# Moving the first prompt tile's load, norm and transposes one stage earlier in a streaming-encoder step

## The chip, the cores and the metric

The kernel is one launch on one core of a Trainium2 chip. The metric is device time in microseconds (us). Five engines run side by side, each with its own queue of instructions in program order: TensorE (PE in the profile; PEld is its weight load), VectorE (DVE), ScalarE (ACT), GpSimd (POOL) and SyncE (SP), which here only issues transfers. An engine waits on semaphores that other engines and transfers raise.

## The reference, cut to what matters

One layer runs on a prompt of 2048 tokens and on a sample of 8 sequences of 16 tokens. Width is 1024, all in float32. The change lies in the second of the three steps of the layer, the attention into 256 memory tokens:

```
def memory_attend(h, mem_k, mem_v, w_xq, w_xo):
    q = (h @ w_xq).reshape(B, T, X_HEADS, X_HEAD_DIM)
    s = jnp.einsum('bqhd,bkhd->bhqk', q, mem_k.astype(q.dtype)).astype(jnp.float32) * (X_HEAD_DIM ** -0.5)
    p = jax.nn.softmax(s, axis=-1).astype(q.dtype)
    o = jnp.einsum('bhqk,bkhd->bqhd', p, mem_v.astype(q.dtype)).reshape(B, T, D_MODEL)
    return o @ w_xo

    x = x + memory_attend(rms_norm(x, g_xattn), mem_k, mem_v, w_xq, w_xo)
    x = x + hier_moe(rms_norm(x, g_ffn), w_rg, b_rg, w_re, b_re, w_eg, w_eu, w_ed)
```

The prompt has one pair of key and value arrays (computed in this launch); the sample has a cached pair for each of its 8 sequences. After the attention each token goes to 2 of 32 experts.

## The kernel before, in words

Tokens are cut into 17 tiles of 128 (NT = 17): tile 16 (PT) is the sample, tiles 0 to 15 are the prompt. The program is a row of stages, each a block in which all five engines run their own code; between stages stands a barrier (L113 to L116), which no engine passes before all have arrived. In order:

- stage **a** (L204): token mixing of all tiles; its result x1 is written to DRAM (`x1_d`, x_scratch in the profile);
- stage **q** (L921): folds the prompt's keys and values into two matrices A and B, and makes the sample's queries;
- stage **s** (L1049): the sample's attention. The cached keys of 8 sequences are loaded, transposed on PE (`turn_keys`, into `psa` and `psb`), copied out by ACT (L1106) and DVE (L1127) and used in `scores(0)` after four sequences and `scores(1)` after eight. The softmax follows on DVE and ACT, then transposes of the probabilities (L1186), `values(0)`, `values(1)` (L1172), and transposes of the result (L1193), which ACT copies to `qT` (L1117). SP issues eight 1 MB key loads (two in stage q), then four value loads, each of which waits for `kb_psum` since it reuses a key buffer, and after `scores(1)` the last four, which land in the buffers of the transposed keys;
- stage **r** (L1220): attention of the prompt, residual, norm, and routing of all 17 tiles in the order `ORDER` (the sample is index 0, prompt tile 0 is index 1). It is a software pipeline over steps s. For index i: SP loads x1 (`load_n`, L1292), ACT squares and sums it (L1395), POOL makes 1/sqrt (`rms1`, L1357 and L1359), ACT scales (L1398, `norm`), PE transposes (`turn_h2`, L1596), DVE applies the gain (`h2T_out`, L1459), and PE multiplies with A (`scores`, L1587, two halves), softmax on DVE and ACT (`exps`, L1414), `turn_p` (L1579) and `residual` (L1613);
- the experts, and the last norm.

Before step s = 0 of stage r the pipeline is filled with the front part of index 1:

```
                    pe.wait_ge(S["iotas"], 3)
                    turn_h2(1)
                    for s in range(NT + 3):
```

and in the same way `norm(1)` on ACT, `rms1(1)` on POOL, `h2T_out(1)` on DVE. At step 0 PE has nothing to do; at step 1 it has `scores(1, 0)`, `turn_h2(2)`, `scores(1, 1)` and `residual(0)`. The index 0 tile needs no norm here, since stages q and s have done its attention.

Of the kernel before, what the change touches and what calls it, by code (L numbers as in the profile page):

```python
# [20 lines left out]
I32 = mybir.dt.int32  # L21
# [5 lines left out]
P = 128  # L27
# [69 lines left out]
def build(nc, I, O):  # L97
# [20 lines left out]
    with top:  # L118
# [929 lines left out]

        with one_stage() as st:  # L1049
# [12 lines left out]
            rc = sb("s_rc", [P, HEADS])  # L1062
            psa = pb("s_psa", [P, 8, P])
# [5 lines left out]
                                            "exp_done rc_done prob_done pT_psum pT_done oT_done").split()}  # L1069
            with nc.Block() as block:  # L1070
                @block.sync
                def _(sp):
                    for i in range(2, SEQS):
                        need(sp, S["kb_psum"], i - 3)
                        load_cache(sp, "cache_mem_k", i, raw[i % 4], key_here[i])
                    for i in range(4):
# [3 lines left out]
                    for i in range(4, SEQS):  # L1080
                        load_cache(sp, "cache_mem_v", i, late[i % 4], value_here[i])

                @block.gpsimd
                def _(pool):
                    pool.memset(only[:], 0.0).then_inc(S["zeroed"], 1)

# [9 lines left out]
                def _(act):  # L1096
# [5 lines left out]
                    for i in range(SEQS):  # L1102
# [3 lines left out]
                        act.activation(KTs[i % 4][:, :, 0:P], psa[:], ACT.Copy).then_inc(S["ka_done"], 1)  # L1106
                    act.wait_ge(S["nb_done"], 1)
# [12 lines left out]
                def _(dve):  # L1120
# [10 lines left out]
                    dve.tensor_scalar(nb[:], mx[:], -SCALE, None, ALU.mult).then_inc(S["nb_done"], 1)  # L1131
                    dve.wait_ge(S["exp_done"], 1)
# [9 lines left out]
                def _(pe):  # L1142
# [39 lines left out]
                    scores(1)  # L1182
                    pe.wait_ge(S["prob_done"], 1)
# [4 lines left out]
                    pe.wait_ge(S["pT_done"], 4)  # L1188
                    values(0)
# [5 lines left out]

        e_stack = ExitStack()
        sbe, _, seme = alloc(e_stack)
        gate_here = seme("gate_here")
        up_here = seme("up_here")
        down_here = seme("down_here")  # L1200
        bidx = sbe("p_bidx", [P, 1])
        first_row = sbe("p_first_row", [P, LANES])
        last_row = sbe("p_last_row", [P, LANES])
        zero = sbe("p_zero", [P, EPL])
        prio = sbe("p_prio", [P, NE])
        load = sbe("p_load", [P, 4, NE])
        slot_base = sbe("p_slot_base", [1, EPL], I32)
# [11 lines left out]
        ORDER = [PT] + list(range(PT))  # L1219
        with one_stage() as st:  # L1220
            sb, pb, sem = alloc(st)
            x1n = [sb(f"r_x1n{i}", [P, D]) for i in range(2)]
# [3 lines left out]
            h2T = [sb(f"r_h2T{i}", [P, KD, P]) for i in range(2)]  # L1226
# [846 lines left out]
```

## Time and profile before

| | us |
|---|---|
| median of 3 runs | 2686.27 (2686.26 to 2688.2) |
| the profiled execution, its own time | 2679.83 |
| its span, first to last instruction | 2678.2 |
| PE busy in it | 2451.4 (92%) |
| stages q (end) and s, 1004 to 1060 | PE busy 39.83 of 56.00 |
| stage r and the planning of the experts, 1060 to 1645 | PE busy 544.83 of 585.00 |
| experts, 1645 to 2590 | PE busy 930.33 of 945.00 |

All times of the trace are counted from the start of the span. A row of a timeline merges neighbouring instructions of one line: its start, the time from the first start to the last end, and in brackets the idle time before it with what ended it. The clock of PE is given as a share of 2.4 GHz: 1.00 is 2.4 and 0.50 is 1.2 GHz.

### The profile page before, as it was taken

The page shows a single profiled execution, that of the slowest core. Times are in us where ns is not written, and L with a number is a line of the kernel's source. Part 1 is how long each engine was busy: PE and PEld are TensorE (multiplying, and loading weights), DVE is VectorE, ACT ScalarE, POOL GpSimd, SP SyncE. Part 2 cuts the span into 40 slices and gives each one's busy share as a digit, 9 for nine tenths or more (in the row PEclk, how much of TensorE's full clock was granted, in tenths as well). Part 3 has the DMA queues.
Part 4 walks back from the last instruction along what each step waited for, and adds up shares of the span by engine and source line. Part 5 has one row for each costly group of instructions (what it writes and reads, how often), then busy time and mean ns, then how long its engine had stood idle before and what let it go on. Part 6 is the DMA issues. An engine that isn't in the chain of part 4 may idle for free. (4 is left out here: it accounts for less than half of the span.)

```text
span 2678.2 us, 31438 instructions
## 1 busy us (share of the span) xinstructions
PE 2451.4 (92%) x9509; PEld 1128.8 (42%) x9510; DVE 843.9 (32%) x2292; ACT 466.7 (17%) x945; POOL 718.5 (27%) x657
## 2 busy tenths in 40 slices
PE   8889999999969695999999995999999999999990
PEld 4444444444434374455555542333333333333330
DVE  1484757566556102233333322011111111111113
ACT  2122222122111022222222211000000000000002
POOL 2354554546434000011111011222222222222224
PEclk9999999999989898999999996999999999999995
DMA  6201110110132407322211134947776479979927
GB/s 217 95 28 59 36 59 35 56 38 36 56 153 102 151 1 275 134 71 69 74 63 63 48 104 164 330 142 235 224 243 220 151 232 324 311 242 312 327 78 282
DMA packets 154265, 390.94 MB, mean 146 GB/s; under 512 B 20738, under 2 KB 21274, under 8 KB 154186
## 3 DMA queue, kind: packets, MB, share of 16 engines
q1 hardware_dynamic: 128178, 339.39, 35.4%
q0 software_dynamic: 19040, 45.23, 7.0%
q10 hardware_dynamic: 6976, 5.42, 0.6%
q8 instruction: 39, 0.64, 0.1%
q14 instruction: 32, 0.26, 0.0%
HBM read 323.53 MB, written 66.70 MB: 146 GB/s over the span
## 5 line engine op out<-in xcount | busy, mean ns | idle before, releaser
L738 PE MATMUL a_psz<-W 128*128 128x512 f32 x1088 | 484.4, 599 | 1.3 <-ACT W L497 1.3
L594 DVE SCALAR_TENSOR_TENSOR yacc<-aext,pcol,yacc 128x256 f32<-128x256 f32 x928 | 369.9, 476 | 0.0
L738 PEld LDWEIGHTS a_psz<-W 128*128 128x128 f32 x1088 | 205.3, 193 | 239.5 <-issue 239.5
L1936 PE MATMUL e_psg<-W,e_xT 128*64 x672 | 298.4, 597 | 3.2 <-DMA W<-in_w_expert_gate 2.2
L1936 PE MATMUL e_psy<-W,e_hT 128*64 x672 | 297.2, 595 | 3.6
L1937 PE MATMUL e_psg<-W,e_xT 128*64 128x512 f32 x672 | 298.4, 597 | 0.0
L1937 PE MATMUL e_psy<-W,e_hT 128*64 128x512 f32 x672 | 297.4, 595 | 0.0
L1937 PE MATMUL e_psu<-W,e_xT 128*64 128x512 f32 x672 | 295.2, 592 | 0.0
L1936 PE MATMUL e_psu<-W,e_xT 128*64 x672 | 295.2, 592 | 0.0
L1763 POOL DMA_INDIRECT x_scratch<-e_y,e_stoken x42 | 69.7, 1660 | 672.8 <-DVE e_token L1860 356.0
L453 POOL TENSOR_TENSOR a_vn<-a_vn,gv 128x512 f32<-128x512 f32 x17 | 242.8, 14282 | 15.2 <-ACT a_vn L542 15.2
L1613 PE MATMUL r_psx<-W 128*128 128x512 f32 x544 | 237.7, 595 | 0.0
L1587 PE MATMUL r_pss<-W,r_h2T 128*128 128x512 f32 x512 | 226.8, 596 | 1.4 <-DVE r_h2T L1459 1.4
L1873 DVE TENSOR_TENSOR e_hb<-e_psu,e_sg 128x256 f32<-128x256 f32 x84 | 31.7, 419 | 552.8 <-PE e_psu L1937 509.8
L1936 PEld LDWEIGHTS e_psg<-W,e_xT 128*64 128x64 f32 x672 | 92.6, 138 | 194.0 <-issue 194.0
L1936 PEld LDWEIGHTS e_psu<-W,e_xT 128*64 128x64 f32 x672 | 92.1, 137 | 188.6 <-issue 188.6
L1936 PEld LDWEIGHTS e_psy<-W,e_hT 128*64 128x64 f32 x672 | 88.6, 137 | 178.3 <-issue 178.3
L1613 PEld LDWEIGHTS r_psx<-W 128*128 128x128 f32 x544 | 102.8, 191 | 123.3 <-issue 123.3
L1587 PEld LDWEIGHTS r_pss<-W,r_h2T 128*128 128x128 f32 x512 | 95.6, 192 | 110.6 <-issue 108.7
L906 PE MATMUL a_psz<-W,a_maT 128*128 128x512 f32 x272 | 122.7, 594 | 5.1 <-ACT a_maT L550 5.1
L906 PE MATMUL a_psz<-W 128*128 128x512 f32 x272 | 122.3, 592 | 0.0
L1885 DVE TENSOR_SCALAR e_y<-e_psy,e_spair 128x512 f32<-128x512 f32 x42 | 31.5, 751 | 265.3 <-PE e_psy L1937 265.3
(316 smaller groups left out, 2560.7 us busy)
## 6 DMA issues: line engine op xcount, KB each, us to landing
W<-in_w_expert_gate SPq DMA_DIRECT2D x32, 2048.0 KB, 10.9
W<-in_w_expert_up SPq DMA_DIRECT2D x32, 2048.0 KB, 10.5
W<-in_w_expert_down SPq DMA_DIRECT2D x32, 2048.0 KB, 10.6
W<-in_x_prompt SPq DMA_DIRECT2D x32, 512.0 KB, 3.9
x_scratch<-W SPq DMA_DIRECT2D x18, 512.0 KB, 3.0
r_x1r<-x_scratch SPq DMA_DIRECT2D x17, 512.0 KB, 4.3
x_scratch<-r_x SPq DMA_DIRECT2D x17, 512.0 KB, 2.9
h_scratch<-r_h SPq DMA_DIRECT2D x17, 512.0 KB, 2.9
```

Source lines behind the costliest of these rows:

```text
L453: pool.tensor_tensor(vn[:], vn[:], gv[:], ALU.mult).then_inc(S["vgain"], 1)
L594: ins = dve.scalar_tensor_tensor(out=out, in0=src, scalar=w, in1=yacc[:, i, :], op0=ALU.mult, op1=ALU.add)
L738: last = pe.matmul(psz[bank][:], hT[t.par][:, k, :], w_in[:, k, COL[bank]:COL[bank] + 512], start=(k == 0), stop=(k == KD - 1))
L906: last = pe.matmul(psz[n][:], (maT[:, k, :] if k < CG else mbl[t.par][:, k - CG, :]), w_out[:, k, 512 * n:512 * n + 512], start=(k == 0), ...
L1587: last = pe.matmul(pss[:, 2 * n:2 * n + 2, :].rearrange("p h n -> p (h n)"), h2T[i % 2][:, k, :], A[:, k, 512 * n:512 * n + 512], start=(k ...
L1613: last = pe.matmul(psx[:, 512 * n:512 * n + 512], (pT if i else qT)[:, c, :], (B if i else w_xo)[:, c, 512 * n:512 * n + 512], start=(c == ...
L1763: pool.indirect_dma_start(out=x2_d.rearrange("t p d -> (t p) d"), out_offset=bass.IndirectOffsetOnAxis(ap=stoken[t.par][:], axis=0), in_=y ...
L1873: dve.tensor_tensor(hb[:, c], psu[:, c], sg[:, c], ALU.mult).then_inc(S["h_done"], 1)
L1885: dve.tensor_scalar(yb[t.par][:, 512:1024], psy[:, 512:1024], spair[t.par][:, 1:2], None, ALU.mult).then_inc(S["y_done"], 1)
L1936: pe.matmul(out[0:HALF, :], xt[:, 0:HALF], W[:, bass.ds(base + at, 512)], start=start, stop=stop)
L1937: return pe.matmul(out[HALF:P, :], xt[:, HALF:P], W[:, at:at + 512], start=start, stop=stop)
```

## The change

The front part of index 1 leaves the head of stage r and stands in stage s. `x1n` and `h2T` are allocated ahead of stage s, in a stack of their own (`r_stack`), and live until the end of stage r. SP issues the loads of `x1n` for index 1 and for index 2 in stage s, between the fourth and the fifth key sequence. ACT squares index 1 after its copy for sequence 3 and scales it in place after its copy for sequence 5; POOL makes the 1/sqrt. PE transposes it after `scores(1)` into `pso`, and DVE applies the gain between the negated maximum and the reciprocal of the sums. `values(0)` waits for that, since it writes `pso`. The norm of index 2 stays in stage r. All counts of semaphores in stage r that spoke of index i are lowered by one; `load_n(3)` no longer waits for a norm. The block of expert arrays (`e_stack`) is moved up unchanged.

```diff
+        r_stack = ExitStack()
+        sbr, _, _ = alloc(r_stack)
+        x1n = [sbr(f"r_x1n{i}", [P, D]) for i in range(2)]
+        h2T = [sbr(f"r_h2T{i}", [P, KD, P]) for i in range(2)]
+        ORDER = [PT] + list(range(PT))
...
                     for i in range(2, SEQS):
                         need(sp, S["kb_psum"], i - 3)
                         load_cache(sp, "cache_mem_k", i, raw[i % 4], key_here[i])
+                        if i == 3:
+                            for j in (1, 2):
+                                sp.dma_start(x1n[j % 2][:], x1_d[ORDER[j], :, :]).then_inc(x1n_here[j % 2], 16)
...
                         load_cache(sp, "cache_mem_v", i, late[i % 4], value_here[i])
+                    sp.wait_ge(x1n_here[0], 16)
...
                     pool.memset(only[:], 0.0).then_inc(S["zeroed"], 1)
+                    pool.wait_ge(S["squares"], 1)
+                    settle(pool)
+                    pool.tensor_scalar(rs[:, 0:1], ss[:], EPS, None, ALU.add).then_inc(S["eps"], 1)
+                    pool.wait_ge(S["eps"], 1)
+                    pool.tensor_tensor(rs[:, 1:2], rs[:, 0:1], mhalf[:], ALU.pow).then_inc(S["rstd"], 1)
...
                         act.activation(KTs[i % 4][:, :, 0:P], psa[:], ACT.Copy).then_inc(S["ka_done"], 1)
+                        if i == 3:
+                            act.wait_ge(x1n_here[1], 16)
+                            act.activation(o_tok[:], x1n[1][:], ACT.Square, scale=1 / 32, accum_out=ss[:]).then_inc(S["squares"], 1)
+                        if i == 5:
+                            act.wait_ge(S["rstd"], 1)
+                            act.wait_ge(S["squares"], 1)
+                            act.activation(x1n[1][:], x1n[1][:], ACT.Copy, scale=rs[:, 1:2]).then_inc(S["normed"], 1)
...
                     dve.tensor_scalar(nb[:], mx[:], -SCALE, None, ALU.mult).then_inc(S["nb_done"], 1)
+                    dve.wait_ge(S["h2_psum"], 1)
+                    dve.tensor_tensor(h2T[1][:], pso[:].rearrange("p (k n) -> p k n", k=KD),
+                                      gcol[:, 8:16].unsqueeze(2).to_broadcast([P, KD, P]), ALU.mult).then_inc(S["h2T_done"], 1)
                     dve.wait_ge(S["exp_done"], 1)
...
                     for i in range(4, SEQS):
                         turn_keys(i)
                     scores(1)
+                    pe.wait_ge(S["normed"], 1)
+                    for k in range(KD):
+                        last = pe.transpose(pso[:, P * k:P * k + P], x1n[1][:, P * k:P * k + P], ident[:])
+                    last.then_inc(S["h2_psum"], 1)
                     pe.wait_ge(S["prob_done"], 1)
                     for h in range(HEADS):
                         for m in range(2):
                             last = pe.transpose(psa[:, 2 * h + m, :], prob[:, h, P * m:P * m + P], ident[:])
                     last.then_inc(S["pT_psum"], 1)
                     pe.wait_ge(S["pT_done"], 4)
+                    pe.wait_ge(S["h2T_done"], 1)
                     values(0)
                     values(1).then_inc(S["o_psum"], 1)
...
                     def load_n(i):
-                        need(sp, S["normed"], i - 2)
+                        need(sp, S["normed"], i - 3)
                         sp.dma_start(x1n[i % 2][:], x1_d[ORDER[i], :, :]).then_inc(x1n_here[i % 2], 16)
...
                     load_r(0)
-                    load_n(1)
-                    load_n(2)
                     load_r(1)
                     load_part(sp, EPL, 0, 0, 0)
                     for s in range(NT + 1):
...
                     def rms1(i):
-                        pool.wait_ge(S["squares1"], i)
-                        need(pool, S["normed"], i - 1)
+                        pool.wait_ge(S["squares1"], i - 1)
+                        need(pool, S["normed"], i - 2)
                         settle(pool)
                         pool.tensor_scalar(rs1[:, 0:1], ss1[:], EPS, None, ALU.add).then_inc(S["eps1"], 1)
-                        pool.wait_ge(S["eps1"], i)
+                        pool.wait_ge(S["eps1"], i - 1)
                         pool.tensor_tensor(rs1[:, 1:2], rs1[:, 0:1], mhalf[:], ALU.pow).then_inc(S["rstd1"], 1)
...
-                    rms1(1)
                     for s in range(NT + 3):
                         if s + 2 < NT:
                             rms1(s + 2)
...
                     def norm(i):
-                        act.wait_ge(x1n_here[i % 2], 16 * ((i + 1) // 2 if i % 2 else i // 2))
-                        need(act, S["h2_turned"], i - 1)
-                        need(act, S["rstd1"], i - 1)
+                        need(act, x1n_here[i % 2], 16 * ((i - 1) // 2))
+                        need(act, S["h2_turned"], i - 2)
+                        need(act, S["rstd1"], i - 2)
                         act.activation(xn, x1n[i % 2][:], ACT.Square, scale=1 / 32, accum_out=ss1[:]).then_inc(S["squares1"], 1)
-                        act.wait_ge(S["rstd1"], i)
-                        act.wait_ge(S["squares1"], i)
+                        act.wait_ge(S["rstd1"], i - 1)
+                        act.wait_ge(S["squares1"], i - 1)
                         act.activation(xn, x1n[i % 2][:], ACT.Copy, scale=rs1[:, 1:2]).then_inc(S["normed"], 1)
...
-                    norm(1)
                     for s in range(NT + 2):
...
                     def h2T_out(i):
-                        dve.wait_ge(S["h2_turned"], i)
+                        dve.wait_ge(S["h2_turned"], i - 1)
                         need(dve, S["s_psum"], i - 2)
                         dve.tensor_tensor(h2T[i % 2][:], pst[:], gcol[:, 8:16].unsqueeze(2).to_broadcast([P, KD, P]), ALU.mult).then_inc(S["h2T_done"], 1)
...
-                    h2T_out(1)
                     for s in range(NT + 3):
...
                         if i == 1:
-                            pe.wait_ge(S["h2T_done"], 2)
+                            pe.wait_ge(S["h2T_done"], 1)
...
                     def scores(i, n):
                         if n == 0:
-                            pe.wait_ge(S["h2T_done"], i)
+                            need(pe, S["h2T_done"], i - 1)
                             need(pe, S["exp_done"], i - 1)
...
                     def turn_h2(i):
-                        pe.wait_ge(S["normed"], i)
+                        pe.wait_ge(S["normed"], i - 1)
                         need(pe, S["pT_done"], i - 2)
...
                     def turn_h3(i):
                         pe.wait_ge(S["h3_done"], i + 1)
-                        need(pe, S["h2T_done"], min(i + 3, NT - 1))
+                        need(pe, S["h2T_done"], min(i + 3, NT - 1) - 1)
                         need(pe, S["pT_done"], min(i + 1, NT - 1))
...
                     pe.wait_ge(S["iotas"], 3)
-                    turn_h2(1)
                     for s in range(NT + 3):
                         if 1 <= s - 1 < NT:
                             turn_p(s - 1)
...
+        r_stack.close()
```

**PE, the end of stage s and the start of stage r.** L1193 and L1239 are the last transposes of stage s, the two branches the way through the barrier. Before:

```order
L1160 MATMUL s_pss<-s_KT,s_only 32x256 x3
L1186 MATMUL s_psa<-ident,s_prob 128x128 x8
...
L1193 MATMUL s_psb<-ident,s_otok 128x128 x8
L1070 UNCONDITIONAL_BRANCH
L1570 UNCONDITIONAL_BRANCH
L1596 MATMUL r_pst<-ident,W 128x128 x8
L1587 MATMUL r_pss<-W,r_h2T 128x512 x8
L1596 MATMUL r_pst<-ident,W 128x128 x8
L1587 MATMUL r_pss<-W,r_h2T 128x512 x8
L1613 MATMUL r_psx<-W 128x512 x16
```

The same place of the changed kernel:

```order
L1201 MATMUL s_pss<-s_KT,s_only 32x256 x3
L1226 MATMUL s_pso<-ident,r_x1n 128x128 x8
L1231 MATMUL s_psa<-ident,s_prob 128x128 x8
...
L1239 MATMUL s_psb<-ident,s_otok 128x128 x8
L1092 UNCONDITIONAL_BRANCH
L1595 UNCONDITIONAL_BRANCH
L1612 MATMUL r_pss<-W,r_h2T 128x512 x8
L1621 MATMUL r_pst<-ident,W 128x128 x8
L1612 MATMUL r_pss<-W,r_h2T 128x512 x8
L1638 MATMUL r_psx<-W 128x512 x16
```

Eight transposes have moved from the head of stage r to the place between the last scores and the transposes of the probabilities; the first thing of stage r is now a half of the scores.

**ACT, the middle of stage s.** The copies of the transposed keys (s_psa) of sequences 0 to 7. Before:

```order
L1106 ACTIVATE W<-s_psa 128x8x128
L1106 ACTIVATE s_KT<-s_psa 128x8x128 x3
L1106 ACTIVATE W<-s_psa 128x8x128
L1106 ACTIVATE s_KT<-s_psa 128x8x128 x3
L1109 ACT_TABLE_LOAD
```

Of the changed kernel:

```order
L1137 ACTIVATE W<-s_psa 128x8x128
L1137 ACTIVATE s_KT<-s_psa 128x8x128 x3
L1140 ACTIVATE s_otok,s_ss<-r_x1n 128x1024
L1137 ACTIVATE W<-s_psa 128x8x128
L1137 ACTIVATE s_KT<-s_psa 128x8x128
L1144 ACTIVATE r_x1n<-r_x1n,s_rs 128x1024
L1137 ACTIVATE s_KT<-s_psa 128x8x128 x2
L1147 ACT_TABLE_LOAD
```

The square stands in the pause of the first scores, the scaling between two key copies, and no further table load comes in.

**SP, the transfers of stage s and of the head of stage r.** Before:

```order
L918 DMA W<-in_cache_mem_k 128x2x1024 x6
L918 DMA W<-in_cache_mem_v 128x2x1024 x5
L918 DMA s_KT<-in_cache_mem_v 128x2x1024 x3
L1070 UNCONDITIONAL_BRANCH
L1288 UNCONDITIONAL_BRANCH
L1296 DMA r_x1r<-x_scratch 128x1024
L1292 DMA r_x1n<-x_scratch 128x1024 x2
L1296 DMA r_x1r<-x_scratch 128x1024
L1216 DMA W<-in_w_expert_gate 128x8x512
L1292 DMA r_x1n<-x_scratch 128x1024 x2
```

Of the changed kernel:

```order
L918 DMA W<-in_cache_mem_k 128x2x1024 x2
L1100 DMA r_x1n<-x_scratch 128x1024 x2
L918 DMA W<-in_cache_mem_k 128x2x1024 x4
L918 DMA W<-in_cache_mem_v 128x2x1024 x5
L918 DMA s_KT<-in_cache_mem_v 128x2x1024 x3
L1092 UNCONDITIONAL_BRANCH
L1318 UNCONDITIONAL_BRANCH
L1326 DMA r_x1r<-x_scratch 128x1024 x2
L1249 DMA W<-in_w_expert_gate 128x8x512
L1322 DMA r_x1n<-x_scratch 128x1024 x2
```

Two loads of 512 KB have moved ahead of four key loads and all value loads; in stage r the expert's 2 MB now stands third.

## Rows read from the trace of the kernel before

**Rows 1.** The page, busy time of each engine, share of the span, instructions.

```profile
PE 2451.4 (92%) x9509; PEld 1128.8 (42%) x9510; DVE 843.9 (32%) x2292; ACT 466.7 (17%) x945; POOL 718.5 (27%) x657
```

**Rows 2.** Windows of stage r: length, five busy times, PE clock, DMA share, GB/s.

```profile
1074.01:1083.70 9.69, 9.69 (x24) 4.69 (x25) 0.00 (x0) 1.15 (x1) 0.79 (x2) 0.81 0.32 108
1083.70:1585.00 501.30, 501.30 (x1645) 259.45 (x1644) 157.97 (x516) 117.32 (x272) 51.86 (x86) 1.00 0.20 69
```

**Rows 3.** Timeline of PE across the barrier between stages s and r.

```profile
1057.26 1.09 PE L1193 MATMUL s_psb<-ident,s_otok 128*128 128x128 f32 x8 [0.80 <-DVE s_otok L1139]
1070.65 1.94 PE L1596 MATMUL r_pst<-ident,W 128*128 128x128 f32 x8 [12.30 <-ACT W L1398]
1074.01 8.98 PE L1587 MATMUL r_pss<-W,r_h2T 128*128 128x512 f32 x16 [1.42 <-DVE r_h2T L1459]
1082.83 1.04 PE L1596 MATMUL r_pst<-ident,W 128*128 128x128 f32 x8
1083.70 7.03 PE L1587 MATMUL r_pss<-W,r_h2T 128*128 128x512 f32 x16
1090.57 13.90 PE L1613 MATMUL r_psx<-W 128*128 128x512 f32 x32
1104.30 1.04 PE L1579 MATMUL r_pst<-ident,W 128*128 128x128 f32 x8
```

**Rows 4.** Timelines of ACT and POOL at the head of stage r.

```profile
1067.11 1.06 ACT L1395 ACTIVATE W<-r_x1n 128x1024 f32<-128x1024 f32 x1 [7.70 <-DMA r_x1n<-x_scratch]
1069.36 1.15 ACT L1398 ACTIVATE W<-r_x1n,r_rs 128x1024 f32<-128x1024 f32 x1 [1.10 <-POOL r_rs L1359]
1060.37 0.30 POOL L1333 TENSOR_SCALAR_AFFINE_SELECT r_lower<-ones 128x128 f32<-128x128 f32 x1
```

**Rows 5.** Timeline of ACT in stage s, the copies of sequences 4 and 6.

```profile
1026.85 1.03 ACT L1106 ACTIVATE W<-s_psa 128x1024 f32<-128x1024 f32 x1 [6.22 <-PE s_psa L1147]
1031.39 1.02 ACT L1106 ACTIVATE s_KT<-s_psa 128x1024 f32<-128x1024 f32 x1 [1.25 <-PE s_psa L1147]
```

**Rows 6.** Timelines of DVE and PE in stage s after the last scores.

```profile
1043.46 0.18 DVE L1133 RECIPROCAL s_rc<-s_sm 128x4 f32<-128x4 f32 x1 [2.00 <-ACT s_prob L1109]
1044.96 1.97 PE L1186 MATMUL s_psa<-ident,s_prob 128*128 128x128 f32 x8 [4.98 <-DVE s_prob L1135]
```

**Rows 7.** Timeline of PE, transposes of key sequences 3 and 7.

```profile
1018.50 1.06 PE L1147 MATMUL s_psa<-ident,W 128*128 128x128 f32 x8 [0.19 <-ACT s_KT L1106]
1032.55 1.06 PE L1147 MATMUL s_psa<-ident,W 128*128 128x128 f32 x8
```

**Rows 8.** Transfers: when SP issued the last key load, and its time to landing.

```profile
1020.75 0.38 SPq L918 DMA_DIRECT2D W<-in_cache_mem_k  x1
W<-in_cache_mem_k SPq DMA_DIRECT2D x1, 1024.0 KB, 8.6
```

**Rows 9.** Transfers of stage r: the expert weights, time to landing, and their issue.

```profile
W<-in_w_expert_gate SPq DMA_DIRECT2D x1, 2048.0 KB, 12.8
1062.24 0.44 SPq L1216 DMA_DIRECT2D W<-in_w_expert_gate  x1
```

**Rows 10.** Windows of the transfers in stage s: at full rate, and two pauses.

```profile
1022.00:1026.00 4.00, 3.88 (x67) 2.66 (x68) 0.00 (x0) 0.00 (x0) 0.00 (x0) 1.00 1.04 413
...
1027.50:1029.50 2.00, 1.67 (x15) 1.36 (x14) 1.23 (x1) 0.76 (x2) 0.00 (x0) 1.00 0.41 63
1039.75:1041.75 2.00, 0.23 (x7) 0.00 (x0) 1.39 (x2) 0.25 (x1) 0.00 (x0) 1.00 0.46 47
```

**Rows 11.** Weight loads of the last values, and landing times of all cache loads.

```profile
1052.76 0.14 PEld L1172 LDWEIGHTS s_pso<-W,s_only 128*32 128x32 f32 x2 [0.52 <-issue]
DMA to landing us min/median/max: 4.9/7.1/11.0
```

**Rows 12.** Windows in which the clock of PE fell, and in which it rose.

```profile
1060.50:1060.75 0.25, 0.00 (x0) 0.00 (x0) 0.00 (x0) 0.00 (x0) 0.25 (x2) 0.89 0.00 0
...
1077.75:1078.00 0.25, 0.25 (x2) 0.12 (x1) 0.00 (x0) 0.00 (x0) 0.00 (x0) 0.97 0.57 213
```

More of the change, by code:

```diff
@@ L1047, in build @@
         kv_stack.close()
+        e_stack = ExitStack()
+        sbe, _, seme = alloc(e_stack)
+        gate_here = seme("gate_here")
+        up_here = seme("up_here")
+        down_here = seme("down_here")
+        bidx = sbe("p_bidx", [P, 1])
+        first_row = sbe("p_first_row", [P, LANES])
+        last_row = sbe("p_last_row", [P, LANES])
+        zero = sbe("p_zero", [P, EPL])
+        prio = sbe("p_prio", [P, NE])
+        load = sbe("p_load", [P, 4, NE])
+        slot_base = sbe("p_slot_base", [1, EPL], I32)
+        r_stack = ExitStack()
[3 more added lines that the diff above has]
+        ORDER = [PT] + list(range(PT))
         with one_stage() as st:
@@ L1062, in build @@
             rc = sb("s_rc", [P, HEADS])
+            ss = sb("s_ss", [P, 1])
+            rs = sb("s_rs", [P, 2])
             psa = pb("s_psa", [P, 8, P])
@@ L1068, in build @@
             S = {n: sem("s_" + n) for n in ("zeroed q_only ka_psum kb_psum ka_done kb_done s_psum o_psum o_done oT_psum max_done nb_done "
-                                            "exp_done rc_done prob_done pT_psum pT_done oT_done").split()}
+                                            "exp_done rc_done prob_done pT_psum pT_done oT_done squares eps rstd normed h2_psum h2T_done").split()}
+            x1n_here = [sem(f"s_x1n_here{i}") for i in range(2)]
             with nc.Block() as block:
@@ L1194, in _ @@
                     last.then_inc(S["oT_psum"], 1)
[L1196 to L1207, printed above, removed]
         def load_part(eng, e, base, n, r):
@@ L1217, in load_part @@
                           I[name][0][bass.ds(e, 1), :, :].rearrange("a (k p) n -> p (a k) n", p=P)).then_inc(here, 16)
-        ORDER = [PT] + list(range(PT))
         with one_stage() as st:
             sb, pb, sem = alloc(st)
-            x1n = [sb(f"r_x1n{i}", [P, D]) for i in range(2)]
             x1r = [sb(f"r_x1r{i}", [P, D]) for i in range(2)]
@@ L1225, in build @@
             h3 = [sb(f"r_h3{i}", [P, D]) for i in range(2)]
-            h2T = [sb(f"r_h2T{i}", [P, KD, P]) for i in range(2)]
             h3T = sb("r_h3T", [P, KD, P])
```

## Prediction, before the changed kernel ran

> **What bounds the kernel now.** I began with the page: PE is busy for 2451.4 us, 92% of the span [rows 1], so what counts is where PE waits, and whether it waits again afterwards for what a change moves. The windows say how stage r runs: from 1083.70 to 1585 PE is busy in 501.30 of 501.30 us at the full clock [rows 2]. So whatever lets this stretch begin earlier is worth its full length at its end. The timeline of PE shows what stands ahead of it [rows 3]: the last transposes of stage s end at 1058.35, then PE is idle for 12.30 us, until 1070.65; eight transposes of index 1 take 1.94 us, then comes a wait of 1.42 us for DVE, and the scores begin at 1074.01. The wait's chain is on the other engines [rows 4]: ACT waits 7.70 us for the load of x1, squares at 1067.11, waits 1.10 us for POOL, and scales until 1070.51. Nothing else feeds PE in that time: step 0 of the pipeline has no work for it. The semaphore that PE waits for first, `iotas` at 3, comes from POOL's third instruction, which ends at 1060.67.
>
> **What the change removes at the head of stage r.** PE's first instruction is now `scores(1, 0)`, and its inputs (A and `h2T[1]`) exist. It waits for `iotas` alone. With 0.15 us for the signal, my estimate from the 0.14 us between ACT's end at 1070.51 and PE's start at 1070.65 [rows 3, 4], it starts at 60.67 + 0.15: 1060.82. In stage r only the transposes and the DVE multiply are gone from PE's path; the rest keeps its order.
>
> How long until `scores(1, 1)` starts, which now is at 1083.70? From the start of `scores(1, 0)` it takes 9.69 us now, at a mean clock of 0.81 [rows 2]. At full clock the same work takes 6.87 (the second half, 1083.70 to 1090.57) plus 0.87 (transposes, 1082.83 to 1083.70), 7.74 us [rows 3]; 1.95 us are lost to the slow clock. The slow clock has a cause in the idle time: it fell around 1060.70, 2.3 us after PE's last work, and rose only around 1077.76 [rows 12]. In the changed kernel the idle time is 1058.35 to 1060.82, 2.47 us, just past the moment at which the clock fell. I take it as fallen and keep the same 1.95 us of loss. Then `scores(1, 1)` starts at 1060.82 + 7.74 + 1.95 = 1070.51 instead of 1083.70: 13.2 us earlier. Bounds for the loss: nothing, if the clock stays up (15.1 us gained); and 3.55 us, if it stays down as long after PE's first work as it did now, 1070.65 to 1077.76, 7.1 us at half speed (11.6 us gained). I choose 1.95 because it was measured on the same instructions.
>
> The Trainium skill, in "TensorE: Matmul & The Clock Gate" under "Part 1: The HAM clock gate", says that the clock follows how busy the engine has recently been and that the number of slow matmuls at a start differs from run to run of one kernel. By that rule the loss would not be a fixed 1.95 us, and the case of no loss (a gain of 15.1 us) is open in some runs; the trace agrees in so far as the clock fell 2.3 us after the work ended and rose 7.1 us after it began again.
>
> **What it adds in stage s.** Everything there must fit beside what bounds that stage, and each piece has a gap:
> - ACT, square: 1.06 us and the reading of the sum, 0.2, in an idle time of 6.22 us ahead of the copy at 1026.85 [rows 4, 5]. Its load was issued around 1011, far ahead. Cost nothing; if the load landed after 1025.6, each us late would cost one, since the key copies queue behind it.
> - ACT, scaling: 1.15 us [rows 4] between the copies of sequences 5 and 6. ACT is idle there for 1.25 us, until 1031.39 [rows 5]. It fits by 0.1 us, and the 1/sqrt is made on POOL, idle, 8 us earlier. Cost 0 to 0.1 us.
> - PE, eight transposes: 1.06 us at full clock [rows 7] in the idle 4.98 us before the transposes of the probabilities [rows 6]. Cost nothing.
> - DVE, the gain: the same instruction takes at most the 1.42 us that PE waited for it [rows 3]; it stands after the negated maximum, in an idle time of 2.00 us before the reciprocal at 1043.46 [rows 6]. `values(0)` waits for it, but also for the probabilities, which come later. Cost nothing; without the cover 1.4 us.
> - The transfers: two loads of 512 KB, 1.05 MB, at 413 GB/s [rows 10]: 2.54 us, in front of four key loads. The last key load was issued at 1020.75 and landed 8.6 us later, 1029.35 [rows 8]; PE turned it at 1032.55 [rows 7]. Pushed by 2.54 us it lands at 1031.89, with 0.66 us to spare. The value loads: the transfers had two pauses of 2 us, at 63 and 47 GB/s, around 1028.5 and 1040.7 [rows 10]. Each could carry 1.7 us of full traffic, 3.4 us together, more than the 2.54 us added. So the last four values, which start only after `scores(1)`, aren't delayed. That matters, since they are what bounds the stage: 4.19 MB from 1041.75 at 413 GB/s end at 1051.9, and PE begins `values(1)` at 1052.76 after 0.52 us of idle with no other input missing [rows 11]. It also means that a faster clock for the transposes and `values(0)` would bring nothing here. Cost of the transfers: nothing, at most their full 2.54 us.
>
> The Trainium skill says in "DMA: Bandwidth & Descriptors", under "Queues, rings and completion order", that on each transfer engine the descriptors of one issuing engine are consumed in ring order. By that rule the two keys issued ahead of the new loads aren't touched, and the later ones are pushed by the whole length; its warning, that completions need not come in order, is the way in which a key could be late all the same.
>
> **What it shifts in stage r.** `norm(2)` finds its x1 there and runs at once, on ACT from about 1060.5, long before PE turns it at 1069.6. SP now issues expert weights third and x1 of index 3 behind them. The weights landed at 1062.24 + 12.8 = 1075.04 [rows 9]; without two tiles ahead of them that is 1072.5, and index 3 lands one tile (1.27 us) later, 1073.8. `norm(3)` is queued ahead of the exponentials of index 1 on ACT. It ends 3.40 us later (1067.11 to 1070.51 in [rows 4]), 1077.2; PE finishes the scores at 1070.51 + 6.87 = 1077.38, so the exponentials aren't held up. Behind that PE has the 13.73 us of `residual(0)` [rows 3] before it needs the probabilities at 1091.1. From the negated maximum to the first transpose takes 3.5 us (1041.46 to 1044.96 [rows 6]), which leaves 10.4 us of spare time. Cost nothing.
>
> **Sum.** 13.2 us off the profiled execution's 2679.83 (span 2678.2 and 1.6 around it): 2666.6. That execution was 6.4 us below the median of the runs shown; against the median it is 2686.27 - 13.2 = **2673.1 us**.
>
> **The rivals.**
> - The clock stays up. The idle time of 2.47 us is shorter than any that now precedes a slow stretch; against it stands the fall 2.3 us after the last work. Gain 15.1 us, 2671.1.
> - Key or value loads come late and stretch stage s. For it: only 0.66 us of room at the last key. Against it: the two pauses. Worst case all 2.54 us, gain 10.7 us, 2675.6.
> - The moved work isn't hidden in stage s: 1.25 + 1.15 + 1.06 + 1.42 = 4.9 us on the path, gain 8.3 us, 2678.0. For it the gap of 1.25 us that takes 1.15 us; against it the other three gaps, all at least 0.5 us wider than their work.
> - The change moves a wait and doesn't remove it: something after stage r is paced by transfers and takes the 13 us back, 2686. Against it: every stage starts at a barrier, and no transfer of a later stage is issued ahead of it except by stage r's own steps.
> - Slower: x1 of index 3 is stuck behind the expert weights, ACT stands before it with the exponentials in its queue, and PE waits for the probabilities of index 1. Break-even needs the spare 10.4 us and the 13.2 us gained to be used up: landing at 1073.8 + 23.6 = 1097.4. If it took 30 us longer than forecast, PE would lose 19.6 and the time be 2692.7. The longest landing in this stretch was 12.8 us [rows 9], so this is unlikely.
>
> **How the numbers follow.** Forecast as worked out (gain about 13.2, slow clock for a while) 0.50; clock stays up 0.22; loads late 0.12; work not hidden 0.06; given back 0.07; slower 0.03. A measurement of this kernel tells from no change about 0.2%, 5.4 us. Faster holds the first four, 0.90; same 0.07; slower 0.03. The likeliest case alone spans 2671.1 to 2674.6 by the bounds of the clock. The range goes up to the unhidden work, 2678, and down to 2667, because one execution of the same kernel was already 6.4 us under its median. What lies outside is the two last rivals and some noise.
>
> **What the next profile would show.** Right: PE idle about 2.5 us between stages s and r, then `scores` first, and PE busy without a gap from there to the end of stage r; the last transposes of stage s at 1057.26 as now; `values(1)` still at about 1052.8; a slow clock in the first microseconds of stage r. Wrong: PE waiting for a key transfer before 1032.55, `values(1)` later than 1052.8, ACT's copies of the keys shifted, or an idle time of PE at the transposes of the probabilities around 1091. A start of stage r later than 1060.1 would mean that stage s grew.

## The result and the profile after

The changed kernel took 2665.91 us (median of 4 runs, 2665.3 to 2670.32) beside 2686.27 us (4 runs, 2686.02 to 2688.2): a ratio of 0.9926, 95% interval 0.9909 to 0.9943. That is 20.4 us faster, with an interval of about 15.3 to 24.4 us. Forecast were 13.2 us and a range of 2667 to 2678; the direction was right, the time lies 1.1 us below the range. Its profiled execution took 2666.03 us (span 2664.4), 13.8 us less than that of the kernel before. So the first question is already in these numbers: profile against profile gives 13.8 us, median against median 20.4.

The timeline of PE after the change, the counterpart of [rows 3]:

```profile
1041.41 1.09 PE L1226 MATMUL s_pso<-ident,r_x1n 128*128 128x128 f32 x8
1046.45 1.97 PE L1231 MATMUL s_psa<-ident,s_prob 128*128 128x128 f32 x8 [3.95 <-DVE s_prob L1176]
1049.27 6.76 PE L1213 MATMUL s_pso<-W,s_only 128*32 128x256 f32 x65 [0.85 <-DVE s_only L1124]
...
1060.11 1.09 PE L1239 MATMUL s_psb<-ident,s_otok 128*128 128x128 f32 x8 [0.82 <-DVE s_otok L1180]
1063.62 7.13 PE L1612 MATMUL r_pss<-W,r_h2T 128*128 128x512 f32 x16 [2.42 <-POOL r_lower L1361]
1070.59 1.04 PE L1621 MATMUL r_pst<-ident,W 128*128 128x128 f32 x8
1071.46 7.03 PE L1612 MATMUL r_pss<-W,r_h2T 128*128 128x512 f32 x16
1078.33 13.90 PE L1638 MATMUL r_psx<-W 128*128 128x512 f32 x32
1092.06 1.04 PE L1604 MATMUL r_pst<-ident,W 128*128 128x128 f32 x8
```

The idle time of 12.30 us between the stages is 2.42 us, ended by POOL's third list (r_lower), and the first scores take 7.13 us, where they took 8.98: there is no slow clock here. After that PE never stops in stage r, which the windows show; compare [rows 2]:

```profile
1063.62:1071.46 7.84, 7.84 (x24) 3.96 (x25) 0.00 (x0) 2.12 (x3) 2.23 (x18) 1.00 0.93 320
1071.46:1573.00 501.54, 501.54 (x1648) 259.72 (x1646) 158.16 (x516) 117.16 (x272) 51.74 (x86) 1.00 0.21 73
```

In stage s one row differs from what was forecast: `values(0)` and one matmul behind it (x65) took 6.76 us, where they took 5.40. PE came to the transposes of the probabilities 34.58 us after the stage's start, as before the change (1046.45 less 1011.87, 1044.96 less 1010.38), but began `values(1)` at 1055.66, 43.8 us after it instead of 42.4. And stage r began 2.90 us later in time than in the profile before (1063.05 beside 1060.15): 1.49 us of that come from stages ahead of stage s, 1.41 from stage s. On ACT the timeline shows the moved pieces, and the first thing queued behind a late transfer in stage r:

```profile
1022.02 1.04 ACT L1140 ACTIVATE s_otok<-r_x1n 128x1024 f32<-128x1024 f32 x1
...
1031.53 1.14 ACT L1144 ACTIVATE r_x1n<-r_x1n,s_rs 128x1024 f32<-128x1024 f32 x1
1032.88 1.02 ACT L1137 ACTIVATE s_KT<-s_psa 128x1024 f32<-128x1024 f32 x1 [0.21 <-PE s_psa L1188]
...
1078.00 1.06 ACT L1422 ACTIVATE W<-r_x1n 128x1024 f32<-128x1024 f32 x1 [10.80 <-DMA r_x1n<-x_scratch]
...
1081.33 0.46 ACT L1441 ACTIVATE W<-r_pss,r_nb 128x256 f32<-128x256 f32 x1
```

The scaling of index 1 leaves ACT still 0.21 us of waiting before the next key copy: it fits. The square of index 3 at 1078.00 waited for its tile, and the exponentials of index 1 queued behind it began at 1081.33. PE didn't notice, since `residual(0)` lasts until 1092.06.

And on DVE the gain stands where it was to stand, with time to spare before the reciprocal:

```profile
1042.87 1.22 DVE L1171 TENSOR_TENSOR r_h2T<-s_pso,gcol 128x1024 f32<-128x1024 f32 x1
1044.96 0.18 DVE L1174 RECIPROCAL s_rc<-s_sm 128x4 f32<-128x4 f32 x1 [0.87 <-ACT s_prob L1147]
```

The transfers, as times from issue to landing: the last key load (issued at 1022.24), and x1 of index 3 (issued at 1064.36).

```profile
W<-in_cache_mem_k SPq DMA_DIRECT2D x1, 1024.0 KB, 11.3
r_x1n<-x_scratch SPq DMA_DIRECT2D x1, 512.0 KB, 13.6
```

The last key took 11.3 us instead of the 8.6 in [rows 8], 2.7 more (forecast 2.54), and landed at 1033.54; PE used it at 1034.05.

### The profile page after: what moved, and what is told of

It is laid out like the page before. It is cut to its first block and busy times, and to the rows that moved or that the text cites. A ratio compares the mean times of both kernels' runs of the same rounds, so it can differ in the third digit from the quotient of the medians.

```text
span 2664.4 us, 31438 instructions
## 1 busy us (share of the span) xinstructions
PE 2451.7 (92%) x9509; PEld 1128.0 (42%) x9510; DVE 843.8 (32%) x2292; ACT 465.9 (17%) x945; POOL 717.8 (27%) x657
```

## The experiments

Ten runs. The two theories, as they stand in the expectations: **A**, the change is worth 13 to 16 us at the head of stage r, and the rest of the first result is spread between executions; **B**, it does something more elsewhere.

The table has been worked out from the timelines of each profile. "Stage s" goes from PE's first key transposes to POOL's first list; "head" from there to the second half of the scores of index 1, behind which PE is busy without a pause. "Scores, first half" is the time of PE's first 16 matmuls of these scores; 7.03 us is what such a half takes at the full clock.

| profile | stage s | head | both | scores, first half |
|---|---|---|---|---|
| before | 49.77 | 23.55 | 73.32 | 8.98 |
| before, again (e1) | 50.72 | 24.15 | 74.87 | 9.83 |
| arrays moved only (e3) | 51.03 | 24.38 | 75.41 | 9.93 |
| loads moved only (e4) | 51.12 | 17.97 | 69.09 | 9.59 |
| changed | 51.18 | 8.41 | 59.59 | 7.13 |
| changed, again (e2) | 51.20 | 8.41 | 59.61 | 7.13 |
| changed, third (e8) | 51.08 | 8.41 | 59.49 | 7.13 |
| start held (e5) | 51.18 | 13.96 | 65.14 | 10.14 |
| loads doubled (e6) | 52.88 | 11.45 | 64.33 | 10.17 |
| PE filled once (e7) | 53.83 | 7.83 | 61.66 | 7.11 |
| lists later (e9) | 51.23 | 7.83 | 59.06 | 7.11 |
| PE filled thrice (e10) | 51.09 | 7.83 | 58.92 | 7.10 |

**e1, the kernel before again.** No edit.

> The kernel before, once more, to see how its own executions spread and where the 6.4 us lie between its profiled execution (2679.83) and its median (2686.27). Theory A (the change is worth its 13 to 15 us at the head of stage r, and the rest of the measured 20.4 us is spread of the executions or of the chips): ratio 1.000, and executions at both about 2680 and about 2686 turn up, so that a large sample's median may lie below 2686. Theory B (the change does something more, some 6 us, outside the head of stage r): executions of before keep to 2686, and 2679.83 was an exception.

Measured: 2684.11 us (11 runs, 2679.49 to 2687.15), ratio 0.9996 (0.9987 to 1.0005). Executions near 2680 and near 2687 both turn up: one execution says little to 5 us. Its profile shows that the first one was a favourable draw at the very place of the change:

```profile
1074.13 1.94 PE L1596 MATMUL r_pst<-ident,W 128*128 128x128 f32 x8 [12.04 <-ACT W L1398]
1077.49 9.83 PE L1587 MATMUL r_pss<-W,r_h2T 128*128 128x512 f32 x16 [1.42 <-DVE r_h2T L1459]
1087.16 1.04 PE L1596 MATMUL r_pst<-ident,W 128*128 128x128 f32 x8
1088.04 7.03 PE L1587 MATMUL r_pss<-W,r_h2T 128*128 128x512 f32 x16
```

The first half of the scores lasts 9.83 us, 2.8 us over the 7.03 at full clock, against 1.95 in [rows 3]. The clock fell later here. The window in which it fell:

```profile
1065.50:1066.00 0.50, 0.00 (x0) 0.00 (x0) 0.00 (x0) 0.00 (x0) 0.41 (x4) 0.89 0.42 156
```

PE's last work of stage s ended at 1062.09. A clock of 0.89 as the mean of half a microsecond puts the fall at about 1065.9, 3.8 us behind that work, and not 2.3 us as in [rows 12].

**e2, the changed kernel again.** No edit.

> The changed kernel, once more. Theory A: 13 to 15 us faster than the kernel before on the same chip, ratio about 0.9947. Theory B: about 20 us faster again, ratio 0.9925. In its profile both expect the scores of index 1 to begin some 13 us earlier after the start of stage r than before; the first microseconds may be at the slow or at the full clock.

Measured: 2670.69 us (5 runs, 2668.18 to 2673.64), ratio 0.9947 (0.9933 to 0.9961), 14.5 us between the medians. Head 8.41, full clock. This is A's value, and B's 0.9925 lies outside the interval.

**e3, only the arrays moved.** The kernel before with:

```diff
+        e_stack = ExitStack()
...
+        r_stack = ExitStack()
+        sbr, _, _ = alloc(r_stack)
+        x1n = [sbr(f"r_x1n{i}", [P, D]) for i in range(2)]
+        h2T = [sbr(f"r_h2T{i}", [P, KD, P]) for i in range(2)]
+        ORDER = [PT] + list(range(PT))
```

> Only the allocations of the change: the expert arrays, x1n and h2T are allocated ahead of stage s, all work stays where it was. Theory A: no change, ratio 1.000, PE's idle time at the head of stage r 12.3 us as before. Theory B, in the form that the places of the arrays in memory matter: about 6 us faster, ratio 0.9976, with PE's idle time at that place unchanged.

Measured: 2684.98 us (11 runs), ratio 0.9998 (0.9989 to 1.0007). No effect of the places in memory is seen, and the interval leaves room for 3 us at most; B's form of it (6 us) falls.

**e4, only the loads moved.** As e3, and:

```diff
+                        if i == 3:
+                            for j in (1, 2):
+                                sp.dma_start(x1n[j % 2][:], x1_d[ORDER[j], :, :]).then_inc(x1n_here[j % 2], 16)
...
-                    load_n(1)
-                    load_n(2)
...
```

> The loads of both x1 tiles move to stage s, all computing stays at the head of stage r. ACT can square from 60.5 instead of 67.1, but POOL is at its index lists until 62.2, so the scaled tile is ready at about 64.4, PE transposes until 66.5, and the scores begin near 67.9 instead of 74.0: a gain of 6.1 us by theory A, ratio 0.9977, less than half of the whole change, the rest being compute that only its move hides. A rival in which the load is all that matters (the compute chain hides behind something) would give the full 13 us or more. Stage s should keep its length, apart from the clock of PE.

Measured: 2677.41 us (7 runs, 2674.38 to 2679.92), ratio 0.9971 (0.996 to 0.9982), 7.8 us. The head is 17.97, 6.2 to 6.4 us shorter than in e1 and e3 (forecast 6.1), and stage s as long as in e3: no cost of the 1 MB of loads is seen there. The timeline:

```profile
1066.00 1.94 PE L1603 MATMUL r_pst<-ident,W 128*128 128x128 f32 x8 [6.11 <-ACT W L1405]
1069.36 9.59 PE L1594 MATMUL r_pss<-W,r_h2T 128*128 128x512 f32 x16 [1.42 <-DVE r_h2T L1466]
1078.79 1.04 PE L1603 MATMUL r_pst<-ident,W 128*128 128x128 f32 x8
```

PE still idles 6.11 us and loses 2.56 us to the slow clock (9.59 against 7.03). The other 9.6 us of the head (17.97 to 8.41) come only with the norm and the transposes.

**e5, PE's start in stage r held back.** The changed kernel with:

```diff
                     pe.wait_ge(S["iotas"], 3)
+                    pe.wait_ge(S["rstd1"], 1)
```

> The changed kernel, but PE starts the scores of index 1 only when POOL has made the 1/sqrt of index 2: 2.55 us later than in the changed kernel, after about 5.0 us of idle instead of 2.4. Theory A (the forecast put the loss by the slow clock at the head of stage r too high, because after 2.4 us of idle the clock mostly stays up): here the clock falls, and from the start of the stage to the second half of the scores of index 1 it takes 8.4 + 2.55 plus 1.7 to 3 us of loss, 12.7 to 14 us. Rival (the clock at this place has nothing to do with the length of the idle time): 11.0 us, full clock. Median about 2672 to 2675 for a changed kernel of about 2668.

```profile
1067.31 10.14 PE L1612 MATMUL r_pss<-W,r_h2T 128*128 128x512 f32 x16 [4.96 <-POOL r_rs L1387]
1077.28 1.04 PE L1621 MATMUL r_pst<-ident,W 128*128 128x128 f32 x8
```

Measured: one execution, 2673.54 us; head 13.96, of which 2.54 is the later start and 3.0 the slow clock (10.14 against 7.13). After 4.96 us of idle the clock had fallen. The head lies in A's range (12.7 to 14) and not at the rival's 11.0. It is one execution, and e6 shows that the length of the idle time alone doesn't decide.

**e6, the loads doubled.** The changed kernel; the second copies go to memory that nothing reads at that time, SP waits for them at the end of the stage, and nothing else is changed.

```diff
+        twin = [W[:, 7168:8192], h2T[0][:].rearrange("p k n -> p (k n)")]
...
+                                sp.dma_start(twin[j % 2], x1_d[ORDER[j], :, :]).then_inc(twin_here[j % 2], 16)
```

> The changed kernel with each of the two x1 tiles loaded twice in stage s (the second copy goes to unused memory): 2.54 us more of transfers in front of the same four keys. Theory A (one pair of tiles fits with 0.5 us to spare at the last key and costs nothing): the last key is now about 2 us late, its transposes begin at 24.3 us after the stage's start instead of 22.2, and the stage grows by 2 to 2.6 us. Rival (transfers in stage s never bound the keys, there is more room than it looks): stage s keeps its 51.2 us.

```profile
1033.96 1.09 PE L1193 MATMUL s_psa<-ident,W 128*128 128x128 f32 x8 [1.71 <-DMA W<-in_cache_mem_k]
...
1036.52 1.09 PE L1193 MATMUL s_psa<-ident,W 128*128 128x128 f32 x8 [0.59 <-DMA W<-in_cache_mem_k]
...
1039.07 1.10 PE L1193 MATMUL s_psa<-ident,W 128*128 128x128 f32 x8 [0.58 <-DMA W<-in_cache_mem_k]
...
1068.39 10.17 PE L1617 MATMUL r_pss<-W,r_h2T 128*128 128x512 f32 x16 [2.42 <-POOL r_lower L1366]
```

Measured: one execution, 2676.33 us. Now three key sequences are late; the last one's transposes begin 24.13 us after the stage's first (forecast 24.3, changed kernel 22.2), and the stage grows by 1.7 us (forecast 2 to 2.6; `values(0)`, 5.39 us here, had the full clock earlier). So the room for the keys was as small as the sum said. The last row is a finding of its own: after the same 2.42 us of idle as in the changed kernel, this time the clock had fallen, and the head took 11.45. PE's last work had ended at 1065.97, and the clock fell at about 1067.7, 1.7 us behind it:

```profile
1067.50:1067.75 0.25, 0.00 (x0) 0.00 (x0) 0.00 (x0) 0.00 (x0) 0.00 (x0) 0.91 0.00 0
1067.75:1068.00 0.25, 0.00 (x0) 0.00 (x0) 0.07 (x1) 0.00 (x0) 0.18 (x2) 0.50 0.00 0
```

So equal idle times at this place can end with either clock. This kernel's stage s differs, though, and all three profiles of the changed kernel itself show the full clock: that the changed kernel too loses the 3.04 us in some executions is not shown.

**e7, PE filled once, lists later.** The changed kernel with 24 transposes whose result nothing reads, and the wait for POOL's lists moved to their first use:

```diff
                     last.then_inc(S["h2_psum"], 1)
+                    for j in range(24):
+                        pe.transpose(psb[:, j % 8, :], x1n[1][:, P * (j % 8):P * (j % 8) + P], ident[:])
...
-                    pe.wait_ge(S["iotas"], 3)
...
+                        if i == 0:
+                            pe.wait_ge(S["iotas"], 3)
                         pe.wait_ge(S["picked"], i + 1)
```

> The changed kernel with two additions: 24 idle transposes into a free part of PSUM after those of index 1, so that PE works through most of the softmax's 3.95 us of idle, and the wait for POOL's lists taken from the head of stage r to the first use of those lists. Theory A (in stage s the slow clock after the softmax costs 1.4 us, until the last values' landing bounds it; the lists cost 0.5 us): transposes of the probabilities 1.06 us instead of 1.97, values(0) about 3.6 instead of 6.8, values(1) at about 42.6 us after the stage's start instead of 44.0, stage r's scores 0.5 us earlier; 2.0 us faster than the changed kernel, ratio to before about 0.9938. Rival (the clock doesn't answer to such filling, or the transfers are later than they look): 0.5 us.

```profile
1048.62 1.09 PE L1233 MATMUL s_psa<-ident,s_prob 128*128 128x128 f32 x8 [1.33 <-DVE s_prob L1176]
1050.56 3.66 PE L1213 MATMUL s_pso<-W,s_only 128*32 128x256 f32 x64 [0.85 <-DVE s_only L1124]
1057.74 0.61 PE L1213 MATMUL s_pso<-W,s_only 128*32 128x256 f32 x1 [3.52 <-DMA s_KT<-in_cache_mem_v]
```

Measured: 2671.58 us (5 runs), ratio 0.995 (0.9937 to 0.9963). A miss in sum: 2.0 us faster than the changed kernel was expected, and it is 3.2 us slower in the mean than e8, which was timed with it (5.2 between the medians). By the trace stage s became 2.7 us longer, and the two stages together 2.2 us longer than in e8. The parts say why. Transposes and `values(0)` ran at full clock as expected (1.09 and 3.66 us), so PE came sooner to its wait for the last values. These were ready 43.7 us after the stage's start, not at the 42.6 expected; PE idled 3.52 us and went into `values(1)` with the slow clock (0.61 us for a matmul that takes 0.38 at full clock). The slow spell had only been moved behind the wait. The lists did what was expected: head 7.83.

**e8, the changed kernel a third time.** No edit.

> The changed kernel a third time, beside more executions of the kernel before. Theory A (the change is worth about 15.5 us at the head of stage r, what differs from that in the first result is spread between executions): ratio about 0.9942, 15 to 16 us. Theory B (about 20 us, the second result being the exception): 0.9925.

Measured: 2666.35 us (6 runs, 2665.83 to 2675.38), ratio 0.994 (0.9925 to 0.9955), 16.1 us by the ratio, 18.0 us between the medians. A's 0.9942 is met, but B's 0.9925 is the edge of the interval: here the timing alone doesn't decide, the profile does. The table's three profiles of the changed kernel agree to 0.12 us in stage s and head together.

**e9, lists later alone.** The changed kernel with the last two pieces of e7's edit.

> The changed kernel with only the wait for POOL's lists taken from the head of stage r to the first use of those lists. PE then starts the scores 0.57 us earlier, after 1.86 us of idle instead of 2.42. Theory A (PE's start there is set by that wait alone): from the start of the stage to the second half of the scores 7.8 us instead of 8.4, always at full clock; stage s unchanged at 51.1; 0.6 us faster than the changed kernel by the trace, which the timing can't resolve: ratio to before 0.993 to 0.995. Rival (something else, such as the fetch of the stage's code, holds PE): 8.4.

```profile
1064.72 7.11 PE L1612 MATMUL r_pss<-W,r_h2T 128*128 128x512 f32 x16 [1.87 <-PEq L116]
```

Measured: 2668.52 us (5 runs), ratio 0.9941 (0.9927 to 0.9954). Head 7.83, as forecast, at the full clock: 0.58 us that the timing can't resolve.

**e10, PE filled thrice.** As e9, with `idle_turns(n, ps)`, a loop of n such transposes:

```diff
+                    idle_turns(24, psb)
...
                     values(0)
+                    idle_turns(28, psb)
                     values(1).then_inc(S["o_psum"], 1)
...
                     last.then_inc(S["oT_psum"], 1)
+                    idle_turns(10, psa)
```

> As the one before, and PE is kept at work with idle transposes in three places of stage s: 24 after those of index 1 (softmax), 28 between values(0) and values(1), where the kernel with one filling waited 3.5 us for the last values and lost the fast clock, and 10 after the last transposes of the stage. Theory A (that loss of 2.7 us in stage s was the slow clock after the wait, and nothing but the landing of the last values then bounds the stage): values(1) begin at 42.6 to 43.9 us after the stage's start and run at full clock, 3.5 us instead of 6.9; stage s takes 50 to 51 us instead of 53.9, and the clock never falls between stages s and r. Ratio to before 0.993 to 0.9945. Rival (the filling itself costs, for instance by slowing the transfers): stage s stays above 52 us.

```profile
1046.42 1.09 PE L1236 MATMUL s_psa<-ident,s_prob 128*128 128x128 f32 x8 [1.33 <-DVE s_prob L1176]
1048.36 3.66 PE L1217 MATMUL s_pso<-W,s_only 128*32 128x256 f32 x64 [0.85 <-DVE s_only L1124]
1051.95 3.27 PE L1208 MATMUL s_psb<-ident,r_x1n 128*128 128x128 f32 x28
1055.50 0.38 PE L1217 MATMUL s_pso<-W,s_only 128*32 128x256 f32 x1 [0.27 <-DMA s_KT<-in_cache_mem_v]
...
1062.95 7.10 PE L1619 MATMUL r_pss<-W,r_h2T 128*128 128x512 f32 x16 [0.80 <-PEq L116]
```

Measured: 2666.63 us (5 runs, 2666.03 to 2669.48), ratio 0.9935 (0.9921 to 0.9948). With the wait filled too, `values(1)` run at full clock (0.38 us each) and stage s is back at 51.09. `values(1)` began 43.7 us after the stage's start in e7 and here alike, so the 2.7 us of e7 were the slow clock. It gains nothing over the changed kernel's 51.2, though: PE had to wait for the last values until 1055.50, and they landed about 1 us later in the stage than in the changed kernel (11.9 us after their issue, 10.8 there). It is the best version that was run; its lead over the changed kernel is 0.7 us in the two stages by the trace, within the timing's uncertainty.

## Why the prediction was right or wrong

**The mechanism and the place were right.** PE's chain at the head of stage r was replaced by scores that begin when POOL's third list is there; the 2.42 us of idle stand against 2.47 forecast. From POOL's first list to the first scores it took 13.86, 13.60 and 13.74 us in the profiles of kernels in which no work was moved (before, e1, e3) and 0.57 us in the three of the changed kernel: 13.0 to 13.3 us less, against 13.19 in the forecast. Stages s and head together take 59.6 us in three profiles of the changed kernel, and 73.3, 74.9 and 75.4 in the three of kernels in which no work was moved: a mean of 14.97 us less.

**The term that was mis-sized is the slow clock at the head of stage r.** The prediction kept "the same 1.95 us of loss" on both sides. On the new side the loss is nought in all three profiles of the changed kernel (7.13 us for the first half); that was the rival "the clock stays up", with 0.22. On the old side 1.95 was low: e1, e3 and e4 show 9.83, 9.93 and 9.59 us, 2.6 to 2.9 of loss. Head alone, that is 24.15 or 24.38 to 8.41, 15.7 to 16.0 us, instead of 13.2. The reason for the choice, that the clock had fallen 2.3 us after PE's last work and the new idle time is 2.47 us, was one reading of a thing that varies: the fall came 2.3 us behind the last work of stage s in the profile before, 3.8 us in e1, 4.2 us in e4 (at about 1064.1) and 1.7 us in e6, and after the same 2.42 us of idle the clock was up three times and down once (e6). The Trainium skill says in "TensorE: Matmul & The Clock Gate", Part 1, that the number of slow matmuls at a start differs from run to run of one kernel. The prediction quoted it, the trace agrees in that the loss differed between executions, and it should have weighed more than a single row.

The counterargument that it gave for the full clock was wrong by its own trace: the new idle time would be "shorter than any that now precedes a slow stretch". In the profile before, PE waits 2.22 us for weights at 1681.54 (the row stands below), and the clock falls right behind that wait:

```profile
1681.75:1682.00 0.25, 0.25 (x2) 0.00 (x0) 0.00 (x0) 0.00 (x0) 0.25 (x1) 0.85 1.04 385
1682.00:1682.25 0.25, 0.25 (x4) 0.15 (x2) 0.00 (x0) 0.00 (x0) 0.25 (x1) 0.50 1.02 377
```

In all twelve profiles that wait was followed by the slow clock nine times, after 2.06 to 2.73 us, and by the full clock three times, after 0.56, 0.97 and 1.70 us. So a loss after 2.42 us was not an unlikely choice; why all three profiles of the changed kernel kept the clock, and e6 did not, stays open.

**Stage s: hidden, as forecast, but for a reason that was half read.** ACT's square and scaling, DVE's gain and PE's eight transposes cost nothing up to the transposes of the probabilities (0.21 and 0.87 us of waiting are left behind them, and PE is there 34.6 us after the stage's start with and without them), and e4 shows the same for the loads. The prediction's sentence that a slower or faster clock in stage s changes nothing, since the last values bound it, held only for the execution it was read in: there `values(0)` took 5.40 us with its first successor and the stage 49.8 us. In the other profiles without fillings or doubled loads the stage took 50.7 to 51.2 us, with `values(0)` at the slow clock for most of its length (6.34 to 6.82). Most of this is no work of the change, since e3, without any moved work, has 51.03; on average the stage is still 0.6 us longer in the three profiles of the changed kernel than in the three without moved work, and whether the change has a part in that was not tested. The sign that the prediction named, a start of stage r later than 1060.1, came true, by the clock in stage s and by the stages ahead of it in about equal parts.

**Transfers.** The last key was forecast to be pushed by 2.54 us and to have 0.66 to spare; it was pushed by 2.7 and had 0.5. e6 shows what lies behind that edge. x1 of index 3 was forecast at 1073.8 on the old clock of the stage; with the 2.9 us by which stage r began later in this execution that is 1076.7, and it landed at 1077.96. The exponentials then were 1.3 us late, and PE's `residual(0)` hid it, as the sum said.

**From 13.2 to the measured 20.4.** Two steps. The clock at the head brings 13.2 to about 15.6 there, and the longer stage s takes 0.6 of it back: 15.0 for both. The rest of the first result did not repeat: later sets gave ratios of 0.9947 and 0.994. They were timed on two different chips, and how much of their difference is the chip's was not separated. Over all sets, 15 executions of the changed kernel have a median of 2668.2 (2665.3 to 2675.4) and 58 of the one before 2685.0 (2678.6 to 2689.1), a difference of the means of 16.0 us. Three of the first 4 runs of the changed kernel lay at its low end (2665.3 to 2666.0) and all 4 of before in its upper half: that part of the 20.4 us is a draw, not the mechanism. The range's lower bound was cut too close as well. It is the likeliest 2673.1 less the 6.4 us known between a profile and a median; the same 6.4 below the rival's 2671.1 would have given 2664.7, and single executions spread over 10 us for either kernel.

About 1 us of the 16.0 isn't accounted for by stages s and head. One place was found where executions differ. These are the first expert matmul that waits for weights, of the kernel before and of the changed one:

```profile
1681.54 0.76 PE L1936 MATMUL e_psg<-W,e_xT 128*64 x1 [2.22 <-DMA W<-in_w_expert_gate]
```

```profile
1669.39 0.64 PE L1961 MATMUL e_psg<-W,e_xT 128*64 x1 [0.56 <-DMA W<-in_w_expert_gate]
```

From there to the start of the last such matmul it takes 912.8 us in the first and 911.1 in the second. In e1 and e2 the wait was 2.73 and 2.46 us and the stretch 912.8; in e8 0.97 and 911.1. The waits of over 2 us are those with the slow clock behind them. Whether the change makes the short wait likelier (two of three profiles of the changed kernel, against none of four of the kernels of before, e1, e3 and e4) was not tested and stays open; of the five edits of the changed kernel only e5 has a wait below 2 us.

## What to carry to other kernels

In this kernel the idle stretch of TensorE at a stage's head had to be priced as the whole interval from the barrier to the first instruction that stays in place, with its slow-clock tail; moving only its load brought 6.3 of 15.9 us, moving the chain the rest. Before a term is taken from a single slow or fast stretch, look at a second execution of the same kernel: here one profile was off by 1.5 to 2.1 us at the place of the change. And before an idle time is filled to keep the clock, look for the next wait behind it: here the slow stretch moved to after that wait.

## What the runs showed of the hardware that was not expected

- The same 2.42 us of idle on PE was followed by the full clock in three executions of the changed kernel (7.13 us for 16 matmuls of 128x512) and by the slow one in e6 (10.17 us). At the first wait for expert weights the clock fell behind nine waits of 2.06 to 2.73 us and behind none of three of 0.56 to 1.70 us.
- At the barrier between stages s and r the clock fell 1.7 us (e6), 2.3 us (before), 3.8 us (e1) and 4.2 us (e4) after PE's last work.
- Filling one idle time with 24 transposes made the stage 2.7 us longer: `values(1)` went from 0.38 to 0.61 us per matmul after a wait of 3.52 us.
- With PE filled, the last 1 MB of values landed 11.9 us (e10) and 12.3 us (e7) after its issue, against 10.6 to 11.2 us in eight profiles without filling (before, e1, e3, e5, changed, e2, e8, e9), at the same place of the same stage. Why the transfer should be slower beside a busier PE was not tested.
- 7.13 against 10.14 us (e5) for one and the same block is the price of a fallen clock at the head of stage r: 3.0 us.
